# A trunk kernel's last residual: routed rows scaled when they are stored, added by DMA, and two low parts made earlier

## The reference

```python
def moe_ffn(x, w_router, b_router, w_gate, w_up, w_down):
    logits = (x @ w_router).astype(jnp.float32) + b_router.astype(jnp.float32)
    top_vals, top_idx = lax.top_k(logits, TOP_K)          # 2 of 8
    weights = jax.nn.softmax(top_vals, axis=-1)
    gates = jnp.sum(jax.nn.one_hot(top_idx, N_EXPERTS, dtype=jnp.float32) * weights[..., None], axis=-2)
    out = jnp.zeros_like(x)
    for e in range(N_EXPERTS):
        out = out + gates[..., e:e + 1].astype(x.dtype) * swiglu(x, w_gate[e], w_up[e], w_down[e])
    return out
...
        h = h + moe_ffn(xn, ...)
    return rms_norm(h, final_norm)
```

## Time and profile before

| what | value |
|---|---|
| median of 3 runs | 1008.78 us |
| lowest, highest | 1007.81, 1008.89 us |
| the profiled execution | 1007.8 us |
| its span, first to last instruction | 1006.0 us |
| TensorE busy | 982.1 us, 98% |
| VectorE busy | 756.4 us, 75% |
| ScalarE busy | 656.1 us, 65% |
| GpSimd busy | 60.6 us, 6% |
| DMA traffic | 287.12 MB, 285 GB/s over the span |
| granted clock of TensorE, mean | 0.997 |

### The profile page before, as it was taken

How to read it: one execution, slowest core, us unless ns; L and a number is a source line. 1 busy time by engine, 2 the same in 40 slices (tenths; PEclk the granted TensorE clock), 3 DMA queues, 4 the chain that set the end, 5 groups by cost and what they waited for, 6 DMA issues and landing times.

```text
span 1006.0 us, 14574 instructions
## 1 busy us (share of the span) xinstructions
PE 982.1 (98%) x4892; PEld 829.4 (82%) x4892; DVE 756.4 (75%) x915; ACT 656.1 (65%) x886; POOL 60.6 (6%) x86
## 2 busy tenths in 40 slices
PE   8999999999999999999999999999999999999995
PEld 6987887888887998988877888888888888888883
DVE  5557665456556566666687989898998989899888
ACT  5555345452445545554596787978879787887964
POOL 1301000000000100000160000000000000000141
PEclk9999999999999999999999999999999999999998
DMA  9843689995566657233669999999999999999992
GB/s 322 237 156 128 189 250 309 289 319 156 200 202 216 220 149 190 103 124 106 219 226 400 399 384 407 378 402 371 390 374 385 406 371 401 373 387 391 381 405 101
DMA packets 150536, 287.12 MB, mean 285 GB/s; under 512 B 12769, under 2 KB 58865, under 8 KB 150498
## 3 DMA queue, kind: packets, MB, share of 16 engines
q1 hardware_dynamic: 147890, 277.64, 77.9%
q0 software_dynamic: 2608, 8.98, 2.6%
HBM read 269.81 MB, written 16.78 MB: 285 GB/s over the span
## 4 chain that ended last, share of the span: by engine, by line
PE 82%; DVE 8%; ACT 3%; DMA 3%; issue 2%; POOL 1%; SPq 1%; DVEq 0%; POOLq 0%; ACTq 0%
PE A L584 20%; PE A L586 20%; PE A L585 20%; PE S L584 4%; PE S L586 4%; PE S L585 4%; DVE lo L1606 3%; PE T L629 2%; DMA raw<-in_moe_w_down 1%; DMA raw<-in_moe_w_up 1%; PE T L1091 1%; ACT hi L1156 1%; PE T L664 1%; PE T L1049 1%; ACT R L1211 1%
## 5 line engine op out<-in xcount | busy, mean ns | idle before, releaser
L1606 DVE TENSOR_TENSOR lo<-raw,hi 128x1024 fp32r<-128x1024 f32 (+4 forms) x532 | 570.8, 1130 | 122.0 <-ACT hi L1156 120.0
L1156 ACT ACTIVATE hi<-raw 128x1024 fp32r<-128x1024 f32 (+4 forms) x532 | 485.2, 981 | 149.6 <-PE A L586 123.3
L584 PE MATMUL A<-lo,xT_hi 128*128 128x512 f32 x820 | 324.1, 395 | 2.5 <-DVE lo L1606 2.4
L586 PE MATMUL A<-hi,xT_hi 128*128 128x512 f32 x820 | 319.9, 390 | 0.0
L585 PE MATMUL A<-hi,xT_lo 128*128 128x512 f32 x820 | 319.6, 390 | 0.0
L584 PEld LDWEIGHTS A<-lo,xT_hi 128*128 128x128 f32 x820 | 154.3, 188 | 35.0 <-DVE lo L1606 3.2
L586 PEld LDWEIGHTS A<-hi,xT_hi 128*128 128x128 f32 x820 | 154.0, 188 | 32.3
L585 PEld LDWEIGHTS A<-hi,xT_lo 128*128 128x128 f32 x820 | 154.3, 188 | 30.2
L584 PE MATMUL S<-lo,xT_hi 128*128 128x512 f32 x224 | 89.1, 398 | 1.0 <-DVE lo L1606 1.0
L586 PE MATMUL S<-hi,xT_hi 128*128 128x512 f32 x224 | 87.5, 391 | 0.0
L585 PE MATMUL S<-hi,xT_lo 128*128 128x512 f32 x224 | 87.4, 390 | 0.0
(11 more groups left out here) (239 smaller groups left out, 884.8 us busy)
## 6 DMA issues: line engine op xcount, KB each, us to landing
raw<-in_moe_w_down SPq DMA_DIRECT2D x64, 896.0 KB, 9.4
raw<-in_moe_w_gate SPq DMA_DIRECT2D x32, 768.0 KB, 8.0
raw<-in_moe_w_up SPq DMA_DIRECT2D x24, 768.0 KB, 7.3
raw<-in_moe_w_gate SPq DMA_DIRECT2D x16, 1024.0 KB, 6.9
raw<-in_moe_w_up SPq DMA_DIRECT2D x32, 512.0 KB, 6.8
raw<-in_moe_w_up SPq DMA_DIRECT2D x16, 1024.0 KB, 8.0
raw<-in_ff_w_gate SPq DMA_DIRECT2D x10, 1024.0 KB, 6.0
raw<-in_ff_w_up SPq DMA_DIRECT2D x10, 1024.0 KB, 7.2
```

The lines of the kernel that those rows point to most:

```text
L584: nc.tensor.matmul(out, stat[0], mov[1], start=start, stop=False)
L586: return nc.tensor.matmul(out, stat[0], mov[0], start=False, stop=stop)
L1156: return nc.scalar.activation(out, in_, ACT.Copy)
L1606: nc.vector.tensor_tensor(piece(lo, SPLIT, u, i), piece(raw, RAW, u, i), piece(hi, SPLIT, u, i).bitcast(F32), ALU.subtract).then_inc(lo_do ...
```

## The change

Three things are changed together.

- The gates go into a new DRAM tensor `gate_slots`, scattered by GpSimd to the same slots as the rows with four indirect DMAs of one value per partition. In each round SyncE loads the 128 gates of an expert into `slot_gate`, and ScalarE multiplies with them in `output_rows`. So the stored rows are already scaled.
- `add_rows` is gone from VectorE. In its place GpSimd issues four accumulating DMAs of 512 KB that add `y_from` to `h` in SBUF, two at a time, the second two after the first have landed. It issues the first when eight low parts of the last round are left to make. VectorE waits for all four before its first `add_output`, and the add_outputs, the squares and the waits for them are reordered: left halves of both tiles first, then right halves.
- VectorE makes parts 2 and 3 of the first expert unit earlier: part 2 before `choose(1)`, part 3 before it waits for the gathered rows of the first expert.

```diff
+    gate_slots = nc.dram_tensor("gate_slots", (BLOCKS * P, 1), F32, kind="Internal").ap()
+    gate_blocks = gate_slots.rearrange("(b p) o -> b p o", p=P)
...
+                    if b == 0:
+                        zeros = sel[:, :].bitcast(F32)
+                        sp.dma_start(gate_slots.rearrange("(p b) o -> p (b o)", p=P), zeros[:, 0:BLOCKS]
+                                     ).then_inc(zero_in, 16)
+                        sp.dma_start(slot_gate[:, :], zeros[:, 0:1]).then_inc(slot_gate_in, 16)
...
                         sp.dma_start(xrow, slots[bass.ds(ve + 2, 1)].rearrange("b p d -> p (b d)")
                                      ).then_inc(xrow_in, 16)
+                        sp.wait_ge(gates_in, 16 * 2 * NT)
+                        sp.dma_start(slot_gate[:, :], gate_blocks[bass.ds(ve + 1, 1)].rearrange("b p o -> p (b o)"),
+                                     allow_slow_non_contiguous=True).then_inc(slot_gate_in, 16)
...
-                act_copy(yrow[:, c * 512:(c + 1) * 512], S[(S_MOE + c) % 2][:, :]
-                         ).then_inc(s_free[(S_MOE + c) % 2], 1)
+                if c == 0:
+                    act.wait_ge(slot_gate_in, ve * 16 + 16)
+                nc.scalar.activation(yrow[:, c * 512:(c + 1) * 512], S[(S_MOE + c) % 2][:, :], ACT.Copy,
+                                     scale=slot_gate[:, 0:1]).then_inc(s_free[(S_MOE + c) % 2], 1)
...
             for n in range(4):
-                t, c = divmod(n, 2)
+                c, t = divmod(n, 2)
                 cols = slice(c * 512, (c + 1) * 512)
                 act.wait_ge(rows_added, n + 1)
...
-            split(U_MOE, 0, (1,))
+            split(U_MOE, 0, (1, 2))
             choose(1)
...
             nc.vector.tensor_tensor(r1[:, 2, :], top[:, :, 1], top[:, :, 0], ALU.subtract).then_inc(ahead_set, 1)
+            split(U_MOE, 0, (3,))
             dve.wait_ge(row_mm, 2)
...
             gathered_lo(T_MOE, 0, (0,))
-            split(U_MOE, 0, (2,))
             gathered_lo(T_MOE, 0, (1,))
-            split(U_MOE, 0, (3,))
             split(U_MOE + 1)
...
-            dve.wait_ge(gates_set, 1)
-            dve.wait_ge(y_back, 16 * 2 * NT)
-            for k in range(2):
-                add_rows(k, 0)
             output_lo(0)
-            add_rows(0, 1)
+            dve.wait_ge(added_in, 16 * 2 * NT)
+            add_output(0, 0)
             output_lo(1)
-            add_output(0, 0)
+            add_output(1, 0)
             add_output(0, 1)
-            add_rows(1, 1)
-            add_output(1, 0)
             add_output(1, 1)
...
+            pool.wait_ge(gates_set, 1)
+            for k in range(2):
+                for t in range(NT):
+                    pool.indirect_dma_start(gate_slots, bass.IndirectOffsetOnAxis(row_to[:, k, t:t + 1], 0),
+                                            gate_row[:, k, t:t + 1], None).then_inc(gates_in, 16)
...
+            pool.wait_ge(lo_done, rounds * (FINE * MU) + n_pieces(U_MOE) - 2 * FINE)
+            step(nc.gpsimd.tensor_tensor(rstd[:, N_FINAL, 0:1], mhalf[:, 0:1], mhalf[:, 0:1], ALU.mult))
+            pool.wait_ge(y_back, 16 * 2 * NT)
+            for k in range(2):
+                if k:
+                    pool.wait_ge(added_in, 16 * NT)
+                for t in range(NT):
+                    pool.dma_start(h[:, t, :], y_from[k][t], accum_op=ALU.add).then_inc(added_in, 16)
             n = N_FINAL
             for t in range(NT):
-                pool.wait_ge(tile_summed, 2 * t + 2)
+                pool.wait_ge(tile_summed, t + 3)
```

More of the change, by code:

```diff
@@ L335, in build @@
         gate_row = sb("gate_row", [P, 2, NT])
+        slot_gate = sb("slot_gate", [P, 1])
         rowf = sb("rowf", [P, 2, 2, NT])
@@ L389, in build @@
         gate_set, rows_added, tile_summed = sem("gate_set"), sem("rows_added"), sem("tile_summed")
-        gates_set = sem("gates_set")
+        gates_set, gates_in = sem("gates_set"), sem("gates_in")
+        slot_gate_in, added_in = sem("slot_gate_in"), sem("added_in")
         last_gained, last_out = sem("last_gained"), sem("last_out")
@@ L2105, in output_lo @@
                                         ALU.subtract).then_inc(y_lo, 1)
-            def add_rows(k, t):
-                step(nc.vector.scalar_tensor_tensor(h[:, t, :], y_from[k][t], gate_row[:, k, t:t + 1],
-                                                    h[:, t, :], ALU.mult, ALU.add))
             def add_output(t, c):
@@ L2315, in _ @@
             nc.gpsimd.tensor_scalar(rowf[:, 1], rowf[:, 0], r1[:, 8, 1:2], None, ALU.is_lt).then_inc(row_to_set, 1)
-            pool.wait_ge(zero_in, 16 * (BLOCKS - 1))
+            pool.wait_ge(zero_in, 16 * BLOCKS)
             pool.wait_ge(y_stored, 16)
```

## The result

The changed kernel takes 1018.81 us (median of 4 runs, 1018.30 to 1020.64) against 1008.32 us for the kernel before in the same session: ratio 1.0107, 95% interval 1.0090 to 1.0125. That is 10.5 us slower. I had forecast 2.1 us slower, 1010.9 us, with a range up to 1013.6 us.

A forecast was written before the change was run, and what follows sets the result against it. TensorE, busy 982.1 of 1006.0 us, was taken as the bound, leaving the expert stage's start and the tail. Gates +0.8, moved parts -1.0 and tail +2.3 gave +2.1 us on 1008.8: 1010.9 us, range 1006.8 to 1013.6.

The forecast's parts named there:

- Rows scaled where stored: Expert stage: ScalarE's scaling and SyncE's issues free, small gate packets cost DMA time; +0.8 us, bounds 0 and 1.6.
- The moved low parts: Start of expert stage: making parts 2 and 3 earlier brings weight loads forward; -1.0 us, bounds 0 and -2.8.
- The wait at 546.95: TensorE's 1.89 us wait in the expert stage's start, forecast some 0.6 us shorter; wrong if gone altogether.
- one of my own signs of being wrong: Prediction wrong if adds landed by 994.6, weights weren't delayed, or TensorE's wait at 546.95 was gone altogether.
- SyncE's load behind part 3: Start of expert stage: a 0.79 MB weight load, issued at 512.60 before, could go at about 508.1.
- The adding DMAs: Tail: a pair of adds takes 7.7 us, double reading setting the pace; the tail's change costs +2.3 us.
- X: Tail: the moment both pairs of adds are in, forecast 997.6, with the end at X + 10.7.
- The weights' delay: Tail: first adds share the engines with the last weights, so TensorE ends 0.65 us later, or 1.35 us.
- The issue of the second DMA: Tail: GpSimd's second adding DMA, possibly slowed under VectorE's splits, is out between 982.3 and 985.5.
- Rival (c): Tail: adds slower still or second issue blocked throughout the splits, pair 10 us; +6.0 us, 1014.8 us; chance 0.15.
- Rival (a): Tail: adds cost no more than copies, TensorE sets X at 994.6; -0.7 us, total 1007.9 us; chance 0.28.
- Rival (b): Expert stage's start gives back all waits, -2.8 us, with TensorE setting X in the tail; 1005.7 us; chance 0.12.

The follow-up runs named there:

- gates of 64 bytes: Changed kernel with each gate scattered as a row of 16 equal values instead of one 4-byte value: 1012.21 us.
- no gates: Changed kernel without the scatter of the gates, the loads of slot_gate and ScalarE's scaling, rows added unscaled: 1012.09 us.
- 512 bytes: Changed kernel with each gate scattered as a row of 128 equal values instead of one 4-byte value: 1012.88 us.
- The two kernels of another session: Changed kernel with plain copies for the adding DMAs, 1013.03 us, and changed kernel with adds begun when no low part is left, 1022.35 us.
- the copies: Changed kernel with its four adding DMAs replaced by plain copies of the same sizes, so h is overwritten: 1013.03 us.
- the adds alone: Changed kernel without gates and with low parts 2 and 3 back at their old places, rows added unscaled: 1012.79 us.

## Why the prediction was wrong, point by point

**The step that failed** is in "Rows scaled where stored": "the 512 four-byte writes of the gates are 0.5 us", from 17 ns a packet. With the reads and the share that would be absorbed, I had +0.8 us, at most 1.6. The runs show 6.6 to 6.7 us for the writes by the medians (changed against gates of 64 bytes, and against no gates; 5.9 against 512 bytes) and nothing measurable for the reads. The two kernels of another session leave only 2.7 and 4.2 us for the whole start (see the copies), still three to five times the 0.8. The 17 ns were an average over packets of 253 bytes (0.96 MB in 3790), which aren't scattered 4-byte writes into DRAM; my upper bound was the same price without absorption, not a dearer kind of packet. And I charged the writes their own time on the engines, when what they did was to slow the loads beside them: a packet took half as long again (77 to 120 ns). The largest error lies here: 5.9 us.

**The moved low parts** were sized about rightly: -1.0 forecast, -0.7 measured on the kernel before at the places of the change and -1.4 directly before the gathered rows, with intervals that reach down to -0.2 in both. The path isn't shown. The wait at 546.95, which I had 0.6 shorter, is gone altogether in the first, one of my own signs of being wrong, and still 1.58 us in the second. I had allowed the second tile's choice 0.1 us of delay; the root step beside the two subtractions took 1.05 us more. SyncE's load behind part 3 went at 509.69 and not at 508.1. In the changed kernel nothing of this gain could be seen, because the weights set the pace there.

**The adding DMAs** went as the forecast said in kind and were 1.2 us dearer in sum: the tail is 3.5 us longer, not 2.3 (the adds alone are 4.1 us slower by the medians). The second pair took 7.1 us (7.7 forecast): half a copy's rate, as assumed, with a fixed part of 2.2 us instead of 2.8 (7.1 less 4.9 of moving at half of 430 GB/s). The Trainium skill's rule in "Collectives: The Full Stack", section "The bandwidth ceiling: the fold count and why AG ≠ RS ≠ AR", that two source reads halve the rate, agrees: the adds moved 199 GB/s on free engines, the copies 381 from 997 to 999. The first pair started at 978.9 on the scale of the kernel before, 1.8 us earlier than I had it, since the low parts ahead of the last eight came 1.4 us earlier on that scale, and landed at 991.2, not 989.9: I had shared the engines as if two-operand packets and loads took turns fairly. X is 998.35 on that scale against 997.6, and the end X + 11.15 against X + 10.7.

**The weights' delay** was 0.65 to 1.35 us in the forecast and 3.05 us in the trace. It hardly shows in the time, as X came later still, but it is why no early start of the adds pays.

**The issue of the second DMA** wasn't blocked: both went out in 1.90 us, by 987.83. But the stretch of splits that I had feared began at 987.59, so this run hardly tried it. Rival (c)'s time of 1014.8 was nearer than mine, for none of its reasons. Rival (a), adds as cheap as copies, has its own test in the copies: their tail is +0.1 us and not -0.7. Rival (b) had the start give back all of its waits; it lost 6.4 us instead.

The sum on the trace: +0.6 that was there before the root step, +6.4 from the start of the stage, where the gates alone are worth 6.6 to 6.7 by the medians and the moved parts nothing under them, and +3.5 from the tail: 10.5 us.

## What to carry to other kernels

Be wary of single words scattered into DRAM, packed 4 bytes apart, beside a stream of loads. Here, rows of 64 bytes with copies of the value cost nothing measurable; GpSimd's 6.29 us for making them were hidden. Read DMA share and GB/s side by side, since a share near 1 says nothing of what arrives. An adding DMA between SBUF places moved at half a copy's rate here and slowed the loads beside it. Starting late doesn't help if all the adds must land first (1022.35 us); what helped was both together, to give the DMAs only what isn't needed first and to start them when the last loads are nearly in (1006.27 us). When the trace of before has no row for an operation, an average price of "small packets" is no upper bound for it.

## What the runs showed that I had not expected

- 512 writes of 4 bytes cut the DMA engines from 389 to 209 GB/s over 14 us at a share of 1.02; 64-byte writes to the same places left 391.
- A stall of TensorE can cost twice. After waits of 1.16 and 1.53 us that ended at 538.32 and 542.87, its granted clock was 0.63 and 0.52 in the two windows from 544 to 548, so mostly at the level of 1.2 GHz, and products followed each other every 0.42 us, not every 0.23. It isn't a rule: in the kernel before, the clock stayed at 1.00 behind the wait of 1.89 us at 546.95.
- GpSimd's 128x1 step took 2.15 us beside VectorE's two-input subtractions in the kernels that have part 2 there, and 1.10 us where only one of them ran. With the clock at 0.50 behind it the first expert product was 2.9 us late (0.6 of them from before), with the clock kept 1.06 us.
- One adding DMA of 512 KB on free engines landed in 4.5 to 4.7 us, a pair in 7.1, a pair of copies in about 4.2.
